# The out projection's weights are loaded, rounded and split during attention instead of at the out projection's start

## The reference

```python
x = layer_norm(x, ln_emb_g, ln_emb_b)
proj = x @ w_in                       # 512 Fourier columns, 512 q, 128 k, 128 v
heads = concatenate([fourier_mix(u, w_fourier),
                     windowed_attention(q, k, v, sink_logits)], axis=-1)
x = layer_norm(DEEPNORM_ALPHA * x + heads @ w_out, ln_mix_g, ln_mix_b)
h = square(relu(x @ w_ff1))
x = layer_norm(DEEPNORM_ALPHA * x + h @ w_ff2, ln_ffn_g, ln_ffn_b)
```

## Time and profile before

| | |
|---|---|
| median of three runs | 2768.51 us |
| the profiled execution | 2769.9 us |
| its span | 2768.2 us |
| PE busy | 2534.2 us, 92% of the span |
| DVE busy | 1414.9 us, 51% |
| ACT busy | 1008.4 us, 36% |
| attention, first scores to last store | 517.85 to 733.6 us |
| out projection, first load issued to last product | 736.8 to some 991 us |

### The profile page before, as it was taken

One profiled execution on the slowest core, in us unless ns is written; L12 is line 12 of the kernel. 1 busy time (PEld: TensorE's weight loads), 2 busy tenths in 40 slices (PEclk: granted clock), 3 DMA queues, 4 the chain that ended last, 5 costly groups with the idle time before them and its releaser, 6 DMA issues. The chain is left out here.

```text
span 2768.2 us, 36960 instructions
## 1 busy us (share of the span) xinstructions
PE 2534.2 (92%) x12672; PEld 2205.0 (80%) x12672; DVE 1414.9 (51%) x2002; ACT 1008.4 (36%) x1720; POOL 222.4 (8%) x259
## 2 busy tenths in 40 slices
PE   3999959599699949999799979989999999999998
PEld 2888858599688837888699979987888888888886
DVE  6322055566556656555566656643354363543634
ACT  2111132588611124444455545543222222222221
POOL 5000020122122210000000000000000000000000
PEclk9999959799899979999899989999999999999999
DMA  5321142532445562223433343326444444454442
GB/s 207 121 106 72 76 147 79 136 76 72 142 133 210 206 271 107 107 109 117 149 127 130 119 160 128 127 93 241 139 147 175 170 170 151 170 178 173 153 167 95
DMA packets 137133, 391.51 MB, mean 141 GB/s; under 512 B 14512, under 2 KB 42160, under 8 KB 127856
## 3 DMA queue, kind: packets, MB, share of 16 engines
q1 hardware_dynamic: 119760, 325.96, 32.8%
q0 software_dynamic: 17312, 64.76, 7.6%
HBM read 275.33 MB, written 115.34 MB: 141 GB/s over the span
## 5 line engine op out<-in xcount | busy, mean ns | idle before, releaser
L57 PE MATMUL e_bank<-e_w_hi,e_h_lo 128*128 128x512 f32 x1280 | 500.9, 391 | 19.8 <-DVE e_w_lo L1572 16.6
L58 PE MATMUL e_bank<-e_w_lo,e_h_hi 128*128 128x512 f32 x1280 | 500.1, 391 | 0.0
L59 PE MATMUL e_bank<-e_w_hi,e_h_hi 128*128 128x512 f32 x1280 | 499.8, 390 | 0.0
L1571 DVE TENSOR_TENSOR e_h_lo<-e_h_raw,e_h_hi 128x512 fp32r<-128x512 f32 x160 | 110.8, 692 | 480.7 <-ACT e_w_hi L1560 480.4
L1558 ACT CAST e_h_hi<-e_h_raw 128x512 fp32r<-128x512 f32 x160 | 99.8, 624 | 613.6 <-PE e_bank L59 606.6
L57 PE MATMUL u_bank<-u_x_hi,u_wa_lo 128*128 128x384 f32 (+1 forms) x768 | 275.5, 359 | 45.9 <-DVE u_wa_lo L1288 31.4
L57 PEld LDWEIGHTS e_bank<-e_w_hi,e_h_lo 128*128 128x128 f32 x1280 | 241.6, 189 | 72.4 <-issue 14.7
L58 PEld LDWEIGHTS e_bank<-e_w_lo,e_h_hi 128*128 128x128 f32 x1280 | 241.6, 189 | 50.3
L59 PEld LDWEIGHTS e_bank<-e_w_hi,e_h_hi 128*128 128x128 f32 x1280 | 241.6, 189 | 50.2
L58 PE MATMUL u_bank<-u_x_lo,u_wa_hi 128*128 128x384 f32 (+1 forms) x768 | 274.7, 358 | 0.0
L59 PE MATMUL u_bank<-u_x_hi,u_wa_hi 128*128 128x384 f32 (+1 forms) x768 | 274.2, 357 | 0.0
(11 more groups left out here) (173 smaller groups left out, 4332.5 us busy)
## 6 DMA issues: line engine op xcount, KB each, us to landing
e_w_raw<-w_ff SPq DMA_DIRECT2D x160, 512.0 KB, 3.6
u_w_raw<-w_ff SPq DMA_DIRECT2D x48, 1024.0 KB, 4.8
e_h_raw<-s_h SPq DMA_DIRECT2D x160, 256.0 KB, 2.7
s_h<-u_h SPq DMA_DIRECT2D x128, 192.0 KB, 1.9
s_xb<-d_mixed SPq DMA_DIRECT2D x10, 1792.0 KB, 5.7
s_h<-u_h SPq DMA_DIRECT2D x64, 256.0 KB, 2.0
s_proj<-a_stage SPq DMA_DIRECT2D x50, 256.0 KB, 2.0
u_x_lo<-s_xb POOLq DMA_DIRECT2D x14, 768.0 KB, 6.5
```

The source lines that it names most:

```text
L57: tensor.matmul(out, w_lo, m_hi, start=first, stop=False, skip_group_check=again)
L58: tensor.matmul(out, w_hi, m_lo, start=False, stop=False, skip_group_check=again)
L59: return tensor.matmul(out, w_hi, m_hi, start=False, stop=last, skip_group_check=again)
L1571: dve.tensor_tensor(h_lo[:, s, :], h_raw[:, s, :], h_hi[:, s, :].bitcast(F32), ALU.subtract)
```

## The change

The eight loads, the eight roundings on ACT and the eight subtractions on DVE leave `mix_out` and go into `attend`. Two tiles for hi and lo of the weights (32 KB per partition each) are allocated around both stages. The raw weights get a ring of two slots in attention instead of eight slots in the out projection. SP issues the first two loads behind the bias, and the others ahead of the stores of blocks 0 to 3, each after the slot's last user is split. ACT and DVE each do one tile at the start of the steps in `W_SLOTS`: (1, 3), (1, 7), (2, 1), (2, 5), (3, 1), (3, 5), (4, 1), (4, 5). PE's product(0) waits once for all eight.

```diff
+        W_SLOTS = ((1, 3), (1, 7), (2, 1), (2, 5), (3, 1), (3, 5), (4, 1), (4, 5))
+        W_BLOCKS = ((2,), (3, 4), (5, 6), (7,))
...
+            def load_w(k):
+                if k >= 2:
+                    sp.wait_ge(w_split, k - 1)
+                sp.dma_start(w_raw[:, k % 2, :], w_out_d[k * P:(k + 1) * P, :]).then_inc(w_ld[k % 2], 16)
+            load_w(0)
+            load_w(1)
+
             def store(b, s, kbs, nxt):
+                if isinstance(b, int) and b < len(W_BLOCKS):
+                    for k in W_BLOCKS[b]:
+                        load_w(k)
                 sp.wait_ge(ot_done, b + 1)
...
+            def rest_w(k):
+                dve.wait_ge(w_hi_done, k + 1)
+                dve.tensor_tensor(w_out_lo[:, k, :], w_raw[:, k % 2, :], w_out_hi[:, k, :].bitcast(F32), ALU.subtract
+                                  ).then_inc(w_split, 1)
...
+                if isinstance(b, int) and (b, h) in W_SLOTS:
+                    rest_w(W_SLOTS.index((b, h)))
                 if h == 0 and nxt:
                     rest_q(b + 1, 1 - s)
...
+            def round_w(k):
+                act.wait_ge(w_ld[k % 2], 16 * (k // 2 + 1))
+                act.copy(w_out_hi[:, k, :], w_raw[:, k % 2, :]).then_inc(w_hi_done, 1)
...
+                if isinstance(b, int) and (b, h) in W_SLOTS:
+                    round_w(W_SLOTS.index((b, h)))
                 if h == 4:
                     sinks(b, s)
...
-            for k in range(KT):
-                sp.dma_start(w_raw[:, k, :], w_out[k * P:(k + 1) * P, :]).then_inc(w_ld[k], 16)
...
             split_heads(0)
-            for k in range(KT):
-                act.wait_ge(w_ld[k], 16)
-                act.copy(w_hi[:, k, :], w_raw[:, k, :]).then_inc(w_hi_done, 1)
             split_heads(1)
...
             rest_of_heads(0)
-            for k in range(KT):
-                dve.wait_ge(w_hi_done, k + 1)
-                dve.tensor_tensor(w_lo[:, k, :], w_raw[:, k, :], w_hi[:, k, :].bitcast(F32),
-                                  ALU.subtract).then_inc(w_split, 1)
             rest_of_heads(1)
...
-                        if n == 0 and h == 0:
-                            pe.wait_ge(w_split, k + 1)
+                        if n == 0 and h == 0 and k == 0:
+                            pe.wait_ge(w_split, KT)
```

More of the change, by code:

```diff
@@ L578, in _, with attend @@
                     channels(then, 1)
-def attend(nc, proj_d, sink, bias_d, ident_d, heads_d):
+def attend(nc, proj_d, sink, bias_d, ident_d, heads_d, w_out_d, w_out):
     AHEAD = {"scores": 6, "bias": 5, "exp": 4, "turn": 3, "high": 2, "rest": 1, "values": 0}
@@ L617, in attend @@
         ot = al.sb("ot", [P, 2, 4, P])
+        w_raw = al.sb("w_raw", [P, 2, D])
         sc = al.ps("sc", [P, 2, 512])
@@ L631, in attend @@
         o_nrm_done = al.sem("o_nrm_done")
+        w_ld, w_hi_done = al.sems("w_ld", 2), al.sem("w_hi_done")
+        w_out_hi, w_out_lo, w_split = w_out
         tr_done, ot_done, ot_st = al.sem("tr_done"), al.sem("ot_done"), al.sems("ot_st", 2)
@@ L940, in mix_out @@
 def mix_out(nc, xn_d, heads_d, w_out, ln_g, ln_b, ident_d, x1_d, xb_d):
+    w_hi, w_lo, w_split = w_out
     with ExitStack() as ctx:
@@ L948, in mix_out @@
         mhalf = al.sb("mhalf", [P, 1])
-        w_raw = al.sb("w_raw", [P, KT, D])
-        w_hi = al.sb("w_hi", [P, KT, D], F32R)
-        w_lo = al.sb("w_lo", [P, KT, D], F32R)
         h_raw = al.sb("h_raw", [P, 2, KT, P])
@@ L968, in mix_out @@
         const_in, const_set = al.sem("const_in"), al.sem("const_set")
-        w_ld, w_hi_done, w_split = al.sems("w_ld", KT), al.sem("w_hi_done"), al.sem("w_split")
         h_ld, h_hi_done, h_split = al.sems("h_ld", 2), al.sem("h_hi_done"), al.sem("h_split")
@@ L1663, in build @@
     fourier(nc, s["proj"], d["w_fourier"], d["chan"], [d["table0"], d["table1"]], s["heads"])
-    attend(nc, s["proj"], d["sink"], d["bias"], d["ident"], s["heads"])
-    mix_out(nc, s["x_norm"], s["heads"], d["w_out"], d["ln_mix_g"], d["ln_mix_b"], d["ident"], s["x1"], s["xb"])
+    with ExitStack() as ctx:
+        w_out = [ctx.enter_context(nc.sbuf_tensor(f"d_w_{part}", [P, KT, D], F32R)) for part in ("hi", "lo")]
+        w_out.append(nc.alloc_semaphore("d_w_split"))
+        attend(nc, s["proj"], d["sink"], d["bias"], d["ident"], s["heads"], d["w_out"], w_out)
+        mix_out(nc, s["x_norm"], s["heads"], w_out, d["ln_mix_g"], d["ln_mix_b"], d["ident"], s["x1"], s["xb"])
     mlp_up(nc, s["xb"], d["w_ff1"], s["h"])
```

## The result

The changed kernel takes 2777.82 us in the median of 8 runs (2774.43 to 2780.37), the kernel before 2768.36 us (2766.96 to 2772.62, 8 runs): ratio 1.0032, 95% interval 1.0023 to 1.0042. It is slower by some 9 us. The profiled execution took 2776.11 us, with a span of 2774.4.

What follows compares the result with a forecast made beforehand. PE was taken as the bound, with ACT close behind in attention. A cost of 12.6 us in attention less a gain of 10.0 at the out projection's start made 2.6 us slower, 2771.1 against the runs' median; range 2762 to 2778.

Steps and rivals of the forecast that it cites:

- the rival of the clock: Attention: PE's pauses make the clock fall four times at narrow slots, 6.8 us, total +9.4, so 2778; chance 15%.
- The cost in attention: Blocks 1 to 4: PE pauses of 4 x 1.2 and 4 x 1.7 us plus 1.0, 12.6 us, bounds 10 to 15.
- The handover that I drew on the times of slot (1, 3): Attention: ACT cast, DVE subtraction, sink minus maximum, bias, then scores; PE stands still for 1.2 us.
- the 1.0 for (1, 7) and (2, 1): Attention: slots two steps apart with the 1.22 us rest of q between, not made up in time; 1.0 us added.
- the first rival: Attention: stalls hidden, only the subtractions' surplus shows, 8 x 0.4 = 3.4 us; total -6.6, so 2762; chance 16%.
- the signs that the prediction named for being wrong: Blocks 1 to 4: clock under 1.00, ACT waiting for DMA; PE's bias waits under 8 us; h(0) landing under 5 us.
- its signs for being right: Eight or more 1 to 2 us bias waits; first matmul 9.4 us after h(0)'s load; product(0) 13.4 us; no w_lo wait.
- The gain at the start: Out projection's start: product(0) ends at 760.0 instead of 769.98, gain 10.0 us, bounds 7.4 to 12.2.
- h(0)'s landing: Out projection's start: load of h(0) lands in 6.9 us instead of 8.85, bounds 5.6 to 8.85.
- product(0): Out projection's first product: 10.88 us plus 2.5 for one cold stretch, 13.4 us instead of 20.25.
- nothing at its end takes it back: Out projection: the whole stage moves forward by the start's gain, 10.0 us, and keeps it to the end.
- The rival with the stalls hidden: Same as the first rival: attention costs only 3.4 us, time 2762; chance 16%.

Runs made afterwards that it cites:

- e3: Changed kernel with ACT's cast of each weight tile two steps ahead of DVE's subtraction: 2771.09 us, ratio 1.0001.
- e2: Changed kernel plus two unused tiles (576 and 7616 bytes per partition) restoring the old offsets of w and h tiles modulo 8192: 2769.31 us, ratio 1.0002.
- e12: Changed kernel plus an unused tile of 7872 bytes ahead of the h tiles, w_hi and h_hi 256 bytes past a multiple of 8192 apart: 2769.85 us, one run.
- e1: Kernel before with only w_hi and w_lo allocated around both stages, all work left in the out projection: 2774.27 us, ratio 1.0018.
- e8: Changed kernel plus one unused tile of 7616 bytes per partition ahead of the h tiles, making h_hi level with w_hi: 2768.47 us, one run.
- e6: Changed kernel with both unused tiles, sixteen pieces of 512 columns in steps 1, 3, 5, 7, cast one step ahead: 2759.29 us, ratio 0.9966.
- e10: As e6, but with the pieces in steps 2, 4, 6 and 7 of blocks 1 to 4: 2759.18 us, ratio 0.9967.

## Why the prediction came out as it did

The forecast was 2771.1, a loss of 2.6 us and no measurable change, with 27% for slower by over 0.2%. It is slower by 0.32%. So the call of no change was wrong, and the time is 7 us above the forecast, 0.2 us inside the upper end of the range. That end was set by the rival of the clock, 2778, and the rival's mechanism gave 1.7 of its 6.8 us. What filled the range up to its end is a term that the prediction didn't have; that the time still lies inside is luck.

**The cost in attention** came to 12.38 us against 12.6. The handover that I drew on the times of slot (1, 3) is what the timeline shows, and e3 took 8.9 us of it away by removing only DVE's wait. But that the two numbers meet is luck too. The 12.6 were to be pauses alone; PE's idle time grew by 8.9. The slots in wide steps made 3.5 us of pauses instead of 5.8 with the 1.0 for (1, 7) and (2, 1), those in narrow ones 5.3 instead of 6.8: 0.90 instead of 1.2 at slot (1, 3), 1.49 instead of 1.7 at (4, 1). At (1, 3) most of the difference is the 0.43 us for sink minus maximum. In the changed kernel it took 0.17 us. Before, POOL's cast of the queries was running beside it:

```profile
533.78 1.04 POOL L729 CAST c_qs<-c_q_raw 128x1024 fp32r<-128x1024 f32 x1 [6.46 <-PE c_sc L867]
```

The other 3.5 us were longer matmuls: 1.7 through the clock's fall, 0.4 in block 0, and 1.4 that stay open, in the stretches with pauses. In the first rival, the sum of 8 x 0.4 is 3.2 and not 3.4.

**The clock** fell once in attention, behind four pauses of 0.9 to 1.6 us. The prediction's rows had one fall behind a pause of 2.5 us, and its rival expected four. The rival's mechanism was there, at one fall instead of four, 1.7 us instead of 6.8. It also means that one of the signs that the prediction named for being wrong came: a granted clock under 1.00 in blocks 1 to 4 (0.50 to 0.73 from 571 to 575). Of its signs for being right, PE waited nine times for the bias more than before, but only three of these waits were over 1 us; no one waited for w_lo; and the first matmul came 10.64 us after the load of h(0), not 9.4.

**The gain at the start** was 8.91 us against 10.0. The term that was off is h(0)'s landing: 8.28 us, not 6.9. I took the median of the earlier trace rows, loads in the middle of the stage, and blamed the weights for the difference to 8.85. But in the eleven kernels e2 to e12, where no weights ran beside it, it took 7.3 to 8.4 us, and in e1, where they did, 8.4. So the first load of the stage is slower for another reason, and the weights' 4 MB cost it 1.5 us at most. The prediction had only gain and shift beside it. In fact the loads of x(0), h(1) and x(1), 512 KB each, are issued on the same queue within 2.4 us of it (748.92, 749.47 and 750.36); whether they are the reason isn't tested. product(0) with 13.14 us against 13.4 was right.

**The missing term** is what made the forecast low: "nothing at its end takes it back" was wrong. Each of the other 19 products became 0.31 us longer, +5.85 us, since the kept tiles lie elsewhere and 64 bytes past a multiple of 256 from the h tiles. e1 shows the cost without anything else of the change, e2 and e8 take it away. I had read the change as one of order and time, and had priced the new address of a tile at nothing without naming it.

So of the sum, +12.4 - 8.9 + 5.9, the first two terms stood in the prediction and the third in none of its rivals. The rival with the stalls hidden was wrong for the change as made; e3 made it come true in attention (3.5 us against its 3.4).

Open is what the 1.4 us of attention's longer matmuls outside the fall and block 0 are, and why the ratios of e6 and e10 show some 2.5 us more than their three spans.

## What to carry to other kernels

Price the loads and the arithmetic of a moved preparation apart: here the loads alone gave some 7 of 8.9 us and cost nothing, while the arithmetic gave some 2 and cost 12, or 1.4 to 1.9 where the cast ran a step ahead of the subtraction and the pieces were small. Between two engines that work in step, a moved pair of operations costs the handover more than the work; put the producer a step or two ahead. And when a change moves a tile that feeds TensorE, compare the time of one product before and after it: an unused tile of a few KB may be worth 5 us.

## What the runs showed of the hardware

- Matmuls of 128x512 fp32r pairs ran at 389 to 390 ns of median duration and 10.88 us a product when the stationary and the moving tile began a multiple of 256 bytes apart, and at 393 to 394 ns and 11.20 us when 64 or 128 bytes were left over: 3%, with nothing in any list of waits.
- The granted clock fell to 0.50 (1.2 GHz) for some 3.4 us from 571.1 on in the changed kernel, behind pauses of PE of 0.91, 1.35, 1.60 and 1.49 us that ended at 554.00, 559.63, 565.45 and 571.06. In e8 it fell at about 568.7, behind the first three alone (0.91, 1.34, 1.59). In e3, with three pauses of 0.37, 0.87 and 0.80 us, it stayed at 1.00.
- A subtraction on DVE with both inputs in SBUF and a cast on POOL held each other up in e10: 1.49 us instead of 0.69 for the subtraction, or 1.49 instead of 1.04 for the cast, whichever came second.
- A load of 512 KB in runs of 512 bytes through the GpSimd queue takes 7.3 to 8.4 us at the head of the stage, and 7.5 in the median of all 20 in the changed kernel.
